# A two-block forward pass: opening stages merged, first seven-product pair reordered, attention's surroundings rewritten

## What is computed

```python
# first block
mod  = silu(c) @ w_ada + b_ada;  mod_c = silu(c_ctx) @ w_ada + b_ada
h_lat = rmsnorm(x, norm1_g) * (1 + sc1) + sh1;   h_ctx likewise with mod_c
u, v, q, k, vv, r, al_f, al_b, ga, gb = split(h @ w_in)
b = bidirectional_gla(q, k, vv, log_sigmoid(al @ w_alpha + b_alpha) / 16)   # chunks of 64
a = chunk_mlp(u, v)                                                        # chunks of 128
x = x + g1 * ((sigmoid(ga) * (a @ w_branch_a) + sigmoid(gb) * (b @ w_branch_b)) @ w_out)
x = rmsnorm(x + g2 * swiglu(modulate(rmsnorm(x, norm2_g))), final_norm_g)
# second block
u, g, q, k, v, z = split(rmsnorm(x) @ w_in_2)
y_a = (rg_lru(conv(u), forward) + rg_lru(conv(u), reverse)) * gelu(g)
y_b = banded_alibi_sink_attention(q, k, v, sink)       # 16 heads of 64, 4 key heads, window 128
x = x + (sigmoid(z0) * y_a + sigmoid(z1) * y_b) @ w_out_2
x = rmsnorm(x + swiglu(rmsnorm(x)))
```

## Time and profile before

| what | value |
|---|---|
| median of three runs | 3408.72 us |
| the profiled execution | 3411.13 us, its span 3409.8 us |
| TensorE busy | 3261.6 us, 96% of the span |
| VectorE, ScalarE, GpSimd busy | 57%, 40%, 11% |
| mean granted clock of TensorE | 0.984 |

### The profile page before, as it was taken

One profiled execution on the slowest core, in us unless ns is written; L12 is line 12 of the kernel. 1 busy time (PEld: TensorE's weight loads), 2 busy tenths in 40 slices (PEclk: granted clock), 3 DMA queues, 4 the chain that ended last, 5 costly groups with the idle time before them and its releaser, 6 DMA issues. The chain is left out here.

```text
span 3409.8 us, 39604 instructions
## 1 busy us (share of the span) xinstructions
PE 3261.6 (96%) x14862; PEld 2651.7 (78%) x14862; DVE 1928.6 (57%) x3098; ACT 1379.7 (40%) x2325; POOL 384.0 (11%) x605
## 2 busy tenths in 40 slices
PE   6999999999999999999999999998888799999998
PEld 3888888878888778888888888877556588888886
DVE  4474433456334387777445454664676587777443
ACT  4593222244333243333233355554575343333221
POOL 0121100002100300000011101111211200001011
PEclk8999999999999999999999999999999899999999
DMA  5366444346543323334852434445744523335752
GB/s 220 107 206 197 134 126 135 124 148 224 190 156 99 126 90 118 105 118 150 254 176 81 164 108 148 134 147 164 163 93 105 185 90 121 112 111 170 240 182 75
DMA packets 228045, 494.14 MB, mean 145 GB/s; under 512 B 21520, under 2 KB 84624, under 8 KB 226320
## 3 DMA queue, kind: packets, MB, share of 16 engines
q1 hardware_dynamic: 147728, 302.30, 28.0%
q0 software_dynamic: 80128, 189.30, 17.0%
HBM read 353.63 MB, written 137.89 MB: 144 GB/s over the span
## 5 line engine op out<-in xcount | busy, mean ns | idle before, releaser
L290 PE MATMUL p<-s_xh,s_wh 128*128 128x512 f32 x2256 | 901.6, 400 | 32.9 <-DVE s_tmp L401 12.3
L291 PE MATMUL p<-s_xl,s_wh 128*128 128x512 f32 x2256 | 885.3, 392 | 0.0
L292 PE MATMUL p<-s_xh,s_wl 128*128 128x512 f32 x2256 | 885.2, 392 | 0.0
L290 PEld LDWEIGHTS p<-s_xh,s_wh 128*128 128x128 f32 x2256 | 428.6, 190 | 127.3 <-issue 22.6
L292 PEld LDWEIGHTS p<-s_xh,s_wl 128*128 128x128 f32 x2256 | 427.5, 190 | 91.2
L291 PEld LDWEIGHTS p<-s_xl,s_wh 128*128 128x128 f32 x2256 | 428.4, 190 | 88.8 <-issue 1.7
L2126 PE MATMUL p<-s_xh,s_wh 128*128 128x512 f32 x1152 | 449.5, 390 | 2.1 <-DVE s_xl L2233 1.1
L2128 PE MATMUL p<-s_xh,s_wl 128*128 128x512 f32 x1152 | 448.2, 389 | 0.0
L2127 PE MATMUL p<-s_xl,s_wh 128*128 128x512 f32 x1152 | 448.2, 389 | 0.0
L250 DVE TENSOR_TENSOR s_wl<-s_ws,s_wh 128x1024 fp32r<-128x1024 f32 x157 | 195.3, 1256 | 232.9 <-ACT s_wh L242 232.6
L2126 PEld LDWEIGHTS p<-s_xh,s_wh 128*128 128x128 f32 x1152 | 216.3, 188 | 48.8 <-issue 4.2
(11 more groups left out here) (381 smaller groups left out, 5102.4 us busy)
## 6 DMA issues: line engine op xcount, KB each, us to landing
d_h<-s_fhl POOLq DMA_DIRECT2D x80, 512.0 KB, 3.2
s_ws<-i_Wf SPq DMA_DIRECT2D x48, 512.0 KB, 4.3
s_qb<-i_Wf SPq DMA_DIRECT2D x40, 512.0 KB, 4.0
s_qb<-i_Wf SPq DMA_DIRECT2D x80, 256.0 KB, 3.1
s_ws<-i_Wf SPq DMA_DIRECT2D x80, 256.0 KB, 2.9
s_aw<-i_adaT SPq DMA_DIRECT2D x32, 512.0 KB, 3.6
s_xh<-d_h POOLq DMA_DIRECT2D x16, 1024.0 KB, 12.1
s_xl<-d_h POOLq DMA_DIRECT2D x16, 1024.0 KB, 14.8
```

The lines of the kernel that those rows point to most:

```text
L290: pe.matmul(o, wh, H[:, k, c:c + n], start=(k == 0), stop=False)
L291: pe.matmul(o, wh, L[:, k, c:c + n], start=False, stop=False)
L292: last = pe.matmul(o, wl, H[:, k, c:c + n], start=False, stop=(k == 7))
```

## The change

- **Opening.** Stages 0 and 1 are merged. SyncE loads the first four raw weight tiles between the modulation's tiles (the third and fourth into `ACC` and `RB`), and x in 16 half tiles, half 1 last. The modulation rows are copied by ScalarE and VectorE, two each. Column sums of half 1, and the spreads of both halves, stand inside the first products. The additions of half 1's squares move from VectorE to GpSimd. The context's k results go through `ACC`, the spread row of half 1 through `RB`.
- **Split jobs.** ScalarE makes a second, unrounded copy of the bank into the second slot and frees the bank; VectorE subtracts between the two slots; GpSimd stores when it is done.
- **First residual stage.** The pairs run (tile pair, half) in the order shown; sums and spread of half 0 move, the hooks of the normalisation take any k.
- **SwiGLU, both blocks.** Sums and spread of half 1 move from the first plain pair to the second; the first seven-product pair runs P3 before P4; high and low parts for it are made in another order; `t3` lies in `RB`.
- **Around attention.** Each merged tile of branch a is stored at its merge, and two z1 stores go behind the loads of keys (`late_stores`). Transposes fill whole banks of 512 columns, copied whole. The second four `wo2` jobs of half 0 keep their result in SBUF ("kept"). After the last scores GpSimd loads the residual and the other four partial results of half 0. In stage 7 SyncE loads half 1's residual after each first addition, the sums move to k = 2 and the spread to k = 6 of the third pair, and weight splits stand elsewhere among VectorE's and ScalarE's work.

The core of the diff:

```diff
+        if 2 <= i < 4:
+            return (ACC, RB)[i - 2][:, 0:n], early_in[i - 2].at(1)
...
+                    p.hi, p.lo = split_hi.due(), split_lo.due()
                     p.slot, p.slot_free = take_slot()
                     store_planned(p.slot, (key, m))
-                    slot_free[p.slot].append(p.ev)
+                    slot_free[p.slot].append(p.lo)
                     p.slot2, p.slot2_free = take_slot()
                     store_planned(p.slot2, (key, m))
+                elif kind == "kept":
...
+        if p.kind == "kept":
+            out, free = p.dst
+            ACW.wait_ge(*free)
+            ac.activation(out, ps, ACT.Copy).then_inc(*evA.up())
...
+            for t in p.slot2_free:
+                ACW.wait_ge(*t)
+            ac.activation(TMP[:, p.slot2, 0:p.n], ps, ACT.Copy, scale=p.scale).then_inc(*evA.up())
...
-        DVW.wait_ge(*p.hi)
-        for t in p.slot2_free:
-            DVW.wait_ge(*t)
-        dv.scalar_tensor_tensor(out=TMP[:, p.slot2, 0:p.n].bitcast(R), in0=B[p.bank][:, 0:p.n], scalar=p.scale, in1=TMP[:, p.slot, 0:p.n],
-                                op0=ALU.mult, op1=ALU.subtract).then_inc(*evD.up())
+        y = TMP[:, p.slot2, 0:p.n]
+        DVW.wait_ge(*p.ev)
+        dv.tensor_tensor(y.bitcast(R), y, TMP[:, p.slot, 0:p.n], ALU.subtract).then_inc(*split_lo.up())
...
+            columns_pe(0)
+            PEW.wait_ge(*mcopy.at(2))
+            PEW.wait_ge(*mcopy_d.at(2))
+            PEW.wait_ge(*ident_in.at(1))
+            for m in range(16):
+                last = pe.transpose(B[0][:, 2 * m:2 * m + 2], mrow[:, m * 128:m * 128 + 128], ident[0:2, 0:2])
+            last.then_inc(*mturn.up())
+            products_pe(firsts[0], {3: lambda: spread_pe(0)})
+            products_pe(firsts[1], {1: lambda: columns_pe(1), 3: lambda: spread_pe(1)})
+            products_pe(firsts[2])
...
+            for k in range(1, 8):
+                POW.wait_ge(*squares.at(16 + k + 1))
+                POW.wait_ge(*added1.at(k - 1))
+                po.tensor_tensor(SQ[1][0], SQ[1][0], SQ[1][k], ALU.add).then_inc(*added1.up())
...
+        pairs = plan_pairs(name, [(0, 0), (0, 1), (1, 0), (1, 1), (2, 0), (3, 0), (2, 1), (3, 1)])
...
+                products_pe(js, {5: lambda: sums_pe(s0)} if (p, h) == (2, 1) else {0: lambda: spread_pe(0, DIA[:, 0, :], s0.diag, n0.q[7])} if (p, h) == (3, 1) else None)
...
+            return PRODUCTS if p.n else PRODUCTS[:5] + PRODUCTS[:4:-1]
...
-                products_pe(e.js, {3: lambda: sums_pe(s1), 6: lambda: spread_pe(1, DIA[:, 1, :], s1.diag, q1[7])} if e is plain[0] else None)
+                products_pe(e.js, {0: lambda: sums_pe(s1), 2: lambda: spread_pe(1, DIA[:, 1, :], s1.diag, q1[7])} if e is plain[1] else None)
...
-            for i in range(4):
-                fold_dve(i + 1)
-                low_dve(i)
+            low_dve(0)
+            fold_dve(2)
+            low_dve(1)
+            second_low_dve()
+            low_dve(2)
+            low_dve(3)
             plain_dve(plain[3])
...
-                    fill_pool(jobs[w])
+                    if w < len(jobs) - 2:
+                        fill_pool(jobs[w])
                     continue
                 for op in w:
-                    if op[0] == "merge" and op[1] < 7:
+                    if op[0] == "merge":
                         store_merged(op[1])
...
-        last.store = lambda: store_merged(7)
+        last.store = late_stores
...
+        items += [("wo2", m, "new first", "kept", (PART[:, m, :], sc_mm.at(128)), "wo2", 1.0, TC) for m in range(4, 8)]
...
+            for i in range(4 * n // 128):
+                a, c, j = i // (n // 128), i % (n // 128), banks_before[u] + i // 4
+                PEW.wait_ge(*divided.at(4 * u + a + 1))
+                if i % 4 == 0:
+                    for t in (turn_free[5 + j] if j < 2 else [copied.at(j - 1)]):
+                        PEW.wait_ge(*t)
+                x = pe.transpose(B[5 + j % 2][:, i % 4 * 128:i % 4 * 128 + 128], PR[u % 3][:, a, c * 128:c * 128 + 128], ident[:])
+                if i % 4 == 3:
+                    x.then_inc(*turned.up())
...
+            for j in range(banks_before[u], banks_before[u + 1]):
+                i = j - banks_before[u]
+                ACW.wait_ge(*turned.at(j + 1))
+                ac.activation(PT[u % 2].rearrange("p a c t -> p (a c t)")[:, 512 * i:512 * i + 512], B[5 + j % 2][:, :], ACT.Copy).then_inc(*copied.up())
...
+            POW.wait_ge(*sc_mm.at(128))
+            for t in written["x2"]:
+                POW.wait_ge(*t)
+            for m in range(8):
+                po.dma_start(X2[:, m, :], dX[m][:, 0:512]).then_inc(*x2_in[m].up())
+                if m < 4:
+                    for t in written[("wo2", m)]:
+                        POW.wait_ge(*t)
+                    po.dma_start(PART[:, m, :], dW2[m][:, 0:512]).then_inc(*part_in[m].up())
...
-            products_pe(pairs[1], {6: lambda: sums_pe(s0)})
-            products_pe(pairs[2], {4: lambda: spread_pe(0, DIA[:, 0, :], s0.diag, n0.q[7])})
+            products_pe(pairs[1])
+            products_pe(pairs[2], {2: lambda: sums_pe(s0), 6: lambda: spread_pe(0, DIA[:, 0, :], s0.diag, n0.q[7])})
```

More of the change, by code:

```diff
@@ L507, in squares_dve @@
-        def squares_dve(j):
-            what, k = sums[j]
-            if k:
-                q = slots.index(j)
-                DVW.wait_ge(*squares.at(j + 1))
-                DVW.wait_ge(*added.now())
-                dv.tensor_tensor(total[what], total[what], TMP[:, q % NT, 0:size[what]], ALU.add).then_inc(*added.up())
-        def modulated_act(what):
-            s, c, H, L, c0 = dst[what]
-            n = size[what]
-            for k in range(8):
-                q = which[what] * 8 + k
-                ACW.wait_ge(*shifted.at(q + 1))
-                ac.activation(H[:, k, c0:c0 + n], TMP[:, q % NT, 0:n], ACT.Identity, bias=shift_of[what][:, k:k + 1]).then_inc(*x_hi.up())
@@ L555, in stage0 @@
-        spread_bank = {"c": 7, 0: 4, 1: 5}
+        column_bank, spread_bank = {"c": 6, 0: 6, 1: 3}, {"c": 4, 0: 5, 1: 3}
         scale_of = {"c": GS[:, 8:16], 0: GS[:, 0:8], 1: GS[:, 0:8]}
         shift_of = {"c": MODC, 0: MOD, 1: MOD}
-        def spread_pe(what, free):
-            n = size[what]
-            PEW.wait_ge(*diag.at(which[what] + 1))
-            for t in free:
-                PEW.wait_ge(*t)
-            pe.matmul(B[spread_bank[what]][:, 0:n], ones[:], DIA[what], start=True, stop=True).then_inc(*spread.up())
@@ new lines, in ada_pe, with columns_pe @@
+        def ada_pe(k):
+            PEW.wait_ge(*silu.at(1))
+            PEW.wait_ge(*ad_in[k].at(1))
+            for c in range(4):
+                last = pe.matmul(B[c][0:2, :], sc2[:, k, :], AD[:, k, c * 512:c * 512 + 512], start=(k == 0), stop=(k == 7))
+            last.then_inc(*ada.up())
+        def columns_pe(what):
+            PEW.wait_ge(*{"c": added.at(7), 0: added.at(14), 1: added1.at(7)}[what])
+            PEW.wait_ge(*const.at(1))
+            if what == 1:
+                PEW.wait_ge(*spread3_free)
+            for j in range(size[what] // 128):
+                c = 4 * which[what] + j
+                last = pe.matmul(B[column_bank[what]][:, c:c + 1], SQ[what][0][:, 128 * j:128 * j + 128], ones[:, 0:1], start=True, stop=True)
+            last.then_inc(*colsum.up())
@@ new lines, in spread_pe, with pe_ @@
+        def spread_pe(what):
+            PEW.wait_ge(*diag.at(which[what] + 1))
+            pe.matmul(B[spread_bank[what]][:, 0:size[what]], ones[:], DIA[what], start=True, stop=True).then_inc(*spread.up())
+        def pe_():
+            for k in range(8):
+                ada_pe(k)
+                if k == 2:
+                    columns_pe("c")
+                if k == 4:
+                    spread_pe("c")
+            columns_pe(0)
[8 more added lines that the diff above has]
+            products_pe(firsts[2])
@@ new lines, in al_dve, with square_dve @@
+        def al_dve(part):
+            p = firsts[part][0]
+            lo = AL[32:64, p.col:p.col + p.n]
+            DVW.wait_ge(*al_hi.at(part + 1))
+            dv.tensor_tensor(lo, B[p.bank][32:64, 0:p.n], lo.bitcast(F), ALU.subtract).then_inc(*al_lo.up())
+        def square_dve(what, k):
+            n = 8 * which[what] + k
+            DVW.wait_ge(*squares.at(n + 1))
+            DVW.wait_ge(*added.now())
+            dv.tensor_tensor(SQ[what][0], SQ[what][0], SQ[what][k], ALU.add).then_inc(*added.up())
@@ L1962, in swiglu @@
             p.units = {}
-            for name in PRODUCTS:
+            for name in products_of(p):
                 u = new_unit(*src[name])
@@ L3039, in stage6 @@
         gated, merged = sig("dv", "gated"), sig("dv", "merged")
+        part_in, x2_in = [sig("out", f"part{m}") for m in range(4)], [sig("out", f"x2_{m}") for m in range(8)]
         y_x = [x_tokens(1)[0] for g in range(16)]
```

704 lines of the change are left out of this document (348 added, 356 removed).

## The result

The changed kernel takes 3349.49 us, the median of four runs (3349.10 to 3351.04); the kernel before, with a fourth run beside it, 3407.64 (3404.79 to 3416.22). The ratio is 0.9826, with a 95% interval from 0.9808 to 0.9844: 58 us faster. Forecast were 3337 with a range from 3321 to 3368. The time is in the range, 12 us above the forecast, and three terms of the sum lie outside their own bounds. Their errors partly cancel, so that the total comes as near as it does is in part luck.

The account below looks back on a forecast made before the run. TensorE works 96% of the span, so only its idle time (about 148 us) and lower-clock time can be won. Terms 19 + 5 + 12 + 15 + 0 + 21 = 72 off 3411.1, median 2.4 lower: 3337 us, range 3321 to 3368.

Parts of the forecast that it names:

- Opening: Kernel start up to the latent products: fewer load gaps and weight waits ahead of the products, 19 us won (11 to 22).
- The lock: Opening: GpSimd's seven additions hold VectorE instructions; 1.3 us charged, at most 9.2; as a rival 3345 us, chance 0.07.
- First residual stage: Third pair of half 0 ahead of half 1: waits go, a P4 wait of about 5 us comes; 5 won (0 to 9).
- Splits: Split jobs: ScalarE's second copy frees the product's bank, so three TensorE waits go; 12 us won (4 to 16).
- allowance: Split jobs: the delay tolerated grows from two jobs (10.8 us) to 17.6 us, just fitting the longest wait.
- less 4 that I leave for ScalarE queueing behind the copies: Split jobs: deduction of 4 us from the 12.3 of waits and 4.0 of clock to be won.
- Rival (d): Split jobs: four slots make ScalarE wait and delay VectorE's recurrence, 20 jobs losing 4.1 us each; 3420 us, chance 0.03.
- (a): In-order queues give a third back, 8 us of it in ScalarE's slot waits in split jobs; 3357 us, chance 0.20.
- Attention's start: Last merged tile stored at its merge, so scores start right after the products: 15 us won (8 to 17).
- rival (c): Attention's start: keys or queries land late, scores start some 12 us later than forecast; 3349 us, chance 0.08.
- Turns: Turned attention weights copied by whole banks: 0 won (-4 to +5), with about the same wait for copies.
- Attention's end: Early residual and partial loads remove 22.0 us of waits and 6.6 of clock; 21 won (13 to 25).

Follow-up runs that it names:

- e8: The kernel before with only the last merged tile stored at its merge and two z1 stores behind the loads of keys: 3401.8 us, ratio 0.9977.
- e6: The changed kernel with sums and spread of half 1 back in the first plain pair in both SwiGLU stages: 3344.9 us.
- e2: The changed kernel with the low parts of the q2 split jobs in four slots of their own: 3335.0 us.
- e11: The changed kernel with values loaded behind the next two weight tiles and the third query load issued by GpSimd ahead of the second pair of keys: 3336.5 us.
- e5: The changed kernel with attention weights turned and copied as before, up to 384 columns a bank, four copies a unit: 3355.3 us.
- e10: The changed kernel with sums and spread of half 1 back in the first plain pair in the last SwiGLU stage only: 3339.1 us.
- e9: The changed kernel run again unaltered: 3346.5 us, ratio to the kernel before 0.9819.
- e12: The changed kernel with own slots for q2 low parts, values behind weights, third queries early, last stage's half 1 spread early: 3316.7 us, ratio to before 0.9731.

## Why the prediction was right and wrong

The direction and the bulk were right: TensorE's single waits were worth what the rows said where they went. By its own steps:

- **Opening, 19 forecast (11 to 22), 21.9 measured** (81.6 less 59.7). The context starts 5.6 us earlier and the latent products another 16.3, for which the step had 16.4. The lock cost what was charged, 1.7 us against 1.3. Of the 5.6, 1.0 is in no term: the first load of the modulation is there after 6.47 us instead of 7.44. Right, at the upper end. Two of the step's terms fall in the next stretch (51.6 against 52.6) and hide each other there: the column sums and the spread that now stand inside it take 2.0 us (0.94 and 1.02), and its first 13 us, which ran at a granted clock of 0.87 before, run at 1.00. The two profiles show another 2.6 us in the stretch to GLA, but e8 without that part has 199.0 there against 202.2, so that is scatter.
- **First residual stage, 5 forecast (0 to 9), 2.3 measured.** The waits 1.33, 2.43 and 3.31 went, 7.1 us, and a wait of 4.26 at P4 came (5 forecast), besides 2.0 at the first product of the pair, 6.2 together. The 2.3 are within the scatter of single profiles: e8, whose first stage is that of the kernel before, has 1601.8 here. The average of the two without this part is 1603.4, that of eleven with it (all but e6) 1600.9. e6 has 1604.0 and its wait of 6.34, so here the later sums were right, by some 3 us at the edge of that scatter.
- **Splits, 12 forecast (4 to 16), nothing measured** (438.4 and 438.8; by the averages of old and new split jobs, 440.3 of three and 436.9 of nine, some 3). The step's "allowance" of four jobs, 17.6 us with a store's landing taken off, is that of the product's bank, and it held: no product waits for its bank. What failed is the "less 4 that I leave for ScalarE queueing behind the copies". Two slots a job in a ring of four give ScalarE only two jobs, 10.8 us, to the same late low part, and the landing of a store comes off these too. ScalarE takes over the wait and passes it on by the gates' banks. Rival (d) had this loop and (a) the place, with 8 us instead of the 12 that it cost; the wait over 10 us came once and did not repeat, as (d) would have had it. e2 confirms it by removal: 14 us.
- **Attention's start, 15 forecast (8 to 17), 2.9 measured alone** (e8). The two waits went as said, and the scores start right behind the products. What the step left out is who is next: it looked at keys and queries, and rival (c) too, but the late transfer was a weight tile, and not TensorE's product but VectorE's place in the queue made it a wait. Rival (c) had the right time, 3349, by chance, and the wrong transfer. With the transfers in a better order (e11) attention is another 9.9 us shorter, so 12.8 of the 15 could be had.
- **Turns, 0 forecast (-4 to +5), 6.6 measured** (e5). The loop of the middle blocks was said to grow by 0.3 us; it shrank by 0.08. The cost of a copy was right: the forecast's 0.44 and 0.55 are busy time over copies, and by that measure the new ones take 48.8 over 88, 0.555 (one by itself lasts 0.593, but successive ones overlap). What was missed is the wait, said to stay about the same: 22.4 us became 16.7. The end blocks were underestimated: 4.5 in the last one.
- **Attention's end, 21 forecast (13 to 25), 20.4 measured.** Right in sum and in the waits that went. But the step took the later spread as given (5.4 and 1.7 back); e10 shows that its reverse wins 6 of these back now that the residual is loaded in time.

In attention, 2.9 by the store and 6.6 by the turns leave some 3 of the 12.4 us; the kept partial results may be in them, which was not tried apart. The columns add up to 60.1 us where 72 was forecast. Against their terms the splits are 12.4 short, attention's start 12.1, the residual stages 3.3 (2.7 and 0.6); the opening is 2.9 over, the turns 6.6, the untried rest of attention 2.9, and the two stretches up to GLA, which had no term, 3.6: 27.8 short and 16.0 over, 11.8 short together.

## What to carry to other kernels

When a buffer is freed earlier by copying out of it, count the ring that the copy goes into, with the landing of its store and with all that stands ahead of that store in the issuing queue: the wait moves to the copying engine and from there to whatever it serves next. When a start is moved forward, list every transfer that now shares the window, weights for later products too, and ask which in-order engine stands behind each. And after loads have been moved up, try again the order that was chosen because they were late.

## What the runs showed of the hardware that was not expected

- A load of 512 KB landed 19.5 us after its issue while keys, values and queries were under way (269 GB/s, DMA share 1.10 in that window), and after 10.5 us when 1 MB on its own queue stood behind instead of ahead of it; the page's median for 512 KB weight tiles elsewhere is 4.2. The order on one queue decided half of it here, but that order is not enough: in the kernel before the same tile stood behind the same 1 MB, with fewer loads of keys and queries still under way, and landed after 10.2 us:

```profile
s_ws<-i_Wz SPq DMA_DIRECT2D x2, 512.0 KB, 10.2
```

- A GpSimd addition of 512 columns more than doubled the VectorE instructions that read two SBUF tiles (0.47 to 1.11 and more) and left as it was one that reads a bank and a single SBUF tile (0.47).
- Of the same code, one stretch of 200 us with turned jobs took between 196.2 and 202.1 us from profile to profile, and between 196.2 and 202.0 over four on one chip (e9 to e12).
